# Recurrent layer: the remainder of every second weight chunk by an adding transfer onto a negated copy

## The reference, cut to what matters

```python
def first_block(x, ...):                       # 512 tokens, width 1024, float32
    for i in range(2):
        h = rms_norm(x, norm_g[i])
        x = x + (lru_mixer if i == 0 else fox_mixer)(h, ...)
    return rms_norm(x, final_g)

def lru_mixer(h, w_in, conv_w, conv_b, wa, ba, wx, bx, a_param, w_out):   # the recurrent layer
    u = h @ w_in                               # 1024 -> 2 * 1536
    xb, gate = u[..., :1536], u[..., 1536:]
    xc = causal_depthwise_conv(xb, conv_w, conv_b)               # 4 taps
    r = sigmoid(block_diag_linear(xc, wa, ba)); i = sigmoid(block_diag_linear(xc, wx, bx))
    log_a = -8.0 * r * softplus(-a_param)
    a = exp(log_a); bterm = sqrt(-expm1(2.0 * log_a)) * (i * xc)
    hs = scan(a * previous + bterm)            # over the 512 tokens
    return (hs * silu(gate)) @ w_out           # 1536 -> 1024
```

## Time and profile before

| | |
|---|---|
| median of 3 runs | 2170.46 us |
| profiled execution, its own time | 2171.6 us |
| its span in the trace | 2169.8 us |
| TensorE busy | 2139.7 us (99%) |
| VectorE busy | 1292.5 us (60%) |
| ScalarE busy | 833.5 us (38%) |
| GpSimd busy | 1.4 us |
| queue of SP: 512 KB weight loads, from issue to landing | 3.3 us (median of 389) |

### The profile page before, as it was taken

One profiled execution on the slowest core, in us unless ns is written; L12 is line 12 of the kernel. 1 busy time (PEld: TensorE's weight loads), 2 busy tenths in 40 slices (PEclk: granted clock), 3 DMA queues, 4 the chain that ended last, 5 costly groups with the idle time before them and its releaser, 6 DMA issues.

```text
span 2169.8 us, 27883 instructions
## 1 busy us (share of the span) xinstructions
PE 2139.7 (99%) x10180; PEld 1853.8 (85%) x10190; DVE 1292.5 (60%) x1866; ACT 833.5 (38%) x1162; POOL 1.4 (0%) x6
## 2 busy tenths in 40 slices
PE   9999999999999999999999999999999999999998
PEld 8787878878888888888888888888888888888887
DVE  8878785768665536656553555665446555553545
ACT  5776574645333313233321323443322234222222
POOL 0000000000000000000000000000000000000000
PEclk9999999999999999999999999999999999999998
DMA  5233222213222232333323323222332233233332
GB/s 180 96 108 98 87 78 78 78 64 117 78 89 87 97 104 100 98 106 97 107 90 115 97 97 107 88 78 81 106 105 98 86 111 114 97 97 107 101 102 78
DMA packets 59512, 211.67 MB, mean 98 GB/s; under 512 B 6737, under 2 KB 7121, under 8 KB 59281
## 3 DMA queue, kind: packets, MB, share of 16 engines
q1 hardware_dynamic: 59040, 208.83, 29.4%
q0 software_dynamic: 224, 1.31, 0.2%
q10 hardware_dynamic: 144, 0.12, 0.0%
HBM read 208.14 MB, written 2.10 MB: 97 GB/s over the span
## 4 chain that ended last, share of the span: by engine, by line
PE 81%; DVE 3%; ACT 2%; issue 1%; DVEq 0%; ACTq 0%
PE bank L673 24%; PE bank L675 24%; PE bank L674 24%; PE bank L668 2%; PE bank L669 2%; PE bank L670 2%; PE bank L853 1%; PE bank L903 1%; PE bank L845 1%; ACT arena L1156 1%; ACT arena L1218 0%; DVE w_lo L1382 0%; PE bank L826 0%; PE bank L931 0%; PE bank L827 0%
## 5 line engine op out<-in xcount | busy, mean ns | idle before, releaser
L1382 DVE TENSOR_TENSOR w_lo<-w_raw,w_hi 128x1024 fp32r<-128x1024 f32 x387 | 466.6, 1222 | 682.2 <-ACT w_hi L1002 681.0
L1002 ACT ACTIVATE w_hi<-w_raw 128x1024 fp32r<-128x1024 f32 x387 | 402.6, 1053 | 848.6 <-PE bank L675 812.2
L673 PE MATMUL bank<-h_hi,w_hi 128*128 128x512 f32 x1788 | 683.3, 382 | 8.9 <-DVE w_lo L1382 3.6
L675 PE MATMUL bank<-h_hi,w_lo 128*128 128x512 f32 x1788 | 679.1, 380 | 0.0
L674 PE MATMUL bank<-h_lo,w_hi 128*128 128x512 f32 x1788 | 679.1, 380 | 0.0
L673 PE MATMUL bank<-y_hi,w_hi 128*128 128x512 f32 x1048 | 399.2, 381 | 5.3 <-DVE w_lo L1382 3.4
L674 PE MATMUL bank<-y_lo,w_hi 128*128 128x512 f32 x1048 | 398.1, 380 | 0.0
L675 PE MATMUL bank<-y_hi,w_lo 128*128 128x512 f32 x1048 | 398.0, 380 | 0.0
L673 PEld LDWEIGHTS bank<-h_hi,w_hi 128*128 128x128 f32 x1788 | 339.0, 190 | 60.5 <-DVE w_lo L1382 7.9
L674 PEld LDWEIGHTS bank<-h_lo,w_hi 128*128 128x128 f32 x1788 | 339.1, 190 | 48.6 <-issue 1.4
L675 PEld LDWEIGHTS bank<-h_hi,w_lo 128*128 128x128 f32 x1788 | 338.9, 190 | 47.8
(11 more groups left out here) (236 smaller groups left out, 1494.4 us busy)
## 6 DMA issues: line engine op xcount, KB each, us to landing
w_raw<-in_stream SPq DMA_DIRECT2D x389, 512.0 KB, 3.3
x<-in_x_t SPq DMA_DIRECT2D x8, 256.0 KB, 7.1
out_t<-x SPq DMA_DIRECT2D x8, 256.0 KB, 2.2
arena<-in_consts POOLq DMA_DIRECT2D x1, 1024.0 KB, 5.2
w_raw<-in_stream SPq DMA_DIRECT2D x2, 256.0 KB, 4.5
arena<-in_positions POOLq DMA_DIRECT2D x1, 256.0 KB, 6.0
vec_t<-in_vecs ACTq DMA_DIRECT2D x1, 112.5 KB, 3.3
ident<-in_consts SPq DMA_DIRECT2D x1, 64.0 KB, 6.8
```

What stands on the lines that cost most here:

```text
L673: pe.matmul(out, w_hi[:, slot, w], streamed(a_h), start=first, stop=False)
L675: mm = pe.matmul(out, w_lo[:, slot, w], streamed(a_h), start=False, stop=last)
L1002: A.activation(w_hi[:, slot, :], w_raw[:, slot, :], ACT.Copy).then_inc(hi_ready, 1)
L1382: V.tensor_tensor(w_lo[:, slot, :], w_raw[:, slot, :], w_hi[:, slot, :].bitcast(F32), ALU.subtract).then_inc(lo_ready, 1)
```

## The change

For 18 chunks of the recurrent layer (`ADDED`: 7, 9, 11, ... 41) VectorE makes no remainder. ScalarE, right behind its rounded copy of the chunk, writes a second one with scale -1.0 into `w_lo` ("minus c" below), and counts `minus_ready`. GpSimd waits for that and issues a transfer from `w_raw` to `w_lo` that adds (`accum_op=ALU.add`), so that `w_lo` holds -rounded + raw. TensorE waits for that transfer (`added_in`, a semaphore for each ring slot) where it waited for `lo_ready`; SP, which reloads `w_raw`, does so too. Its first 48 loads are now written out one by one, since their waits differ. The counts of `lo_ready` are lower by the chunks left out.

```diff
+ADDED = range(7, 43, 2)
...
+            single = -(-ADDED.stop // RING) + 1
+            for c in range(RING, single * RING):
+                last = c - RING
+                if last in ADDED:
+                    sp.wait_ge(added_in[c % RING], 16 * transfers(last))
+                else:
+                    sp.wait_ge(lo_ready, last + 1 - sum(a < last for a in ADDED))
+                sp.dma_start(w_raw[:, c % RING, :], stream[c, :, :]).then_inc(raw_loaded[c % RING], 16)
+            with sp.Fori(single, rounds) as r:
...
+            for i, c in enumerate(ADDED):
+                slot = c % RING
+                pool.wait_ge(minus_ready, i + 1)
+                pool.dma_start(w_lo[:, slot, :].bitcast(F32), w_raw[:, slot, :], accum_op=ALU.add)\
+                    .then_inc(added_in[slot], 16)
...
+            def weights_ready(n):
+
+                if by_transfer(T, n):
+                    c = T.fixed["chunk"] + n
+                    pe.wait_ge(added_in[c % RING], 16 * transfers(c))
+                else:
+                    pe.wait_ge(lo_ready, subtracted(T, n + 1))
...
                     A.activation(w_hi[:, slot, :], w_raw[:, slot, :], ACT.Copy).then_inc(hi_ready, 1)
+                    if by_transfer(T, n):
+                        A.activation(w_lo[:, slot, :], w_raw[:, slot, :], ACT.Copy, scale=-1.0)\
+                            .then_inc(minus_ready, 1)
...
                 for n, slot in list(split_slots(T, step))[which]:
 
+                    if by_transfer(T, n):
+                        continue
                     dve.wait_ge(hi_ready, T.value("chunk", n + 1))
```

More of the change, by code:

```diff
@@ L499, in build @@
         hi_ready = sem("hi_ready")
+        minus_ready = sem("minus_ready")
+        added_in = [sem(f"added_in{i}") for i in range(RING)]
         lo_ready = sem("lo_ready")
@@ L534, in norm_banks, with by_transfer, transfers, subtracted @@
             return bank[own], bank[own + 1]
+        def by_transfer(T, n):
+            return not T.loops and T.fixed["chunk"] + n in ADDED
+        def transfers(c):
+            return sum(a <= c and a % RING == c % RING for a in ADDED)
+        def subtracted(T, n):
+            before = sum(T.loops != [] or a < T.fixed["chunk"] + n for a in ADDED)
+            return T.value("chunk", n - before)
         def wait(eng, s, value):
@@ L558, in _ @@
             rounds = (n_chunks + AHEAD) // RING
-            with sp.Fori(1, rounds) as r:
+            single = -(-ADDED.stop // RING) + 1
[7 more added lines that the diff above has]
+            with sp.Fori(single, rounds) as r:
                 for slot in range(RING):
-                    sp.wait_ge(lo_ready, r * RING + (slot - RING + 1))
+                    sp.wait_ge(lo_ready, r * RING + (slot - RING + 1 - len(ADDED)))
                     sp.dma_start(w_raw[:, slot, :], stream[r * RING + slot, :, :])\
@@ L565, in _ @@
             for c in range(rounds * RING, n_chunks + AHEAD):
-                sp.wait_ge(lo_ready, c - RING + 1)
+                sp.wait_ge(lo_ready, c - RING + 1 - len(ADDED))
                 sp.dma_start(w_raw[:, c % RING, :], stream[c, :, :]).then_inc(raw_loaded[c % RING], 16)
@@ L640, in product @@
                     else:
-                        pe.wait_ge(lo_ready, T.value("chunk", c + 1))
+                        weights_ready(c)
                     if step.args.get("apart") and c == step.chunks - 1:
@@ L753, in gates @@
                 pe.wait_ge(a_lo, T.mark["xc", b])
-                pe.wait_ge(lo_ready, T.value("chunk", 1))
+                weights_ready(0)
                 for n in range(4):
```

## The result

| | before | changed |
|---|---|---|
| median | 2170.32 us (2169.27 to 2170.83, 4 runs) | 2181.26 us (2178.2 to 2181.69, 4 runs) |
| profiled execution, its span | 2169.8 us | 2179.7 us |
| VectorE, ScalarE busy | 1292.5, 833.5 us | 1273.2, 850.5 us |

The ratio is 1.0048 (1.0036 to 1.006): slower by 10.9 us, with 2181 predicted. Measured again later beside experiment e9, the same kernel took 2178.57 us (2177.75 to 2180.9, 5 runs; ratio 1.0043, 1.0029 to 1.0057) with a span of 2176.0.

What follows compares the result with a forecast made beforehand. A chain between ScalarE and VectorE, not TensorE, was taken to set the pace from chunk 17 to 39. Chain 4.3, last link 4.9 and clock 1.1 gave +10.3 us, so 2181 us (2179 to 2185, chance 0.52; range 2174 to 2200).

Steps and rivals of the forecast that it cites:

- point 3: Ahead of chunk 17: lo 11 leaves the second convolution's path, -2.2; minus 7 and minus 13 cost +1.9; together -0.3 us.
- point 4: TensorE, late at chunk 17, holds back the next evacuation by some 1 us: +0.9 us.
- Point 1: Negated copies of chunks 17, 23, 27, 33 and 37 are on the chain, 0.96 us each: +4.8 us; others hidden.
- spot (a): Place in a gate round where ScalarE's copies stand directly ahead of Tanh and Exp while VectorE waits, 2.55 us idle.
- Point 2: Subtractions leaving VectorE help only where it is late: -1.0 us at lo 35, -0.1 at 19 and 29 together, others 0.
- D: Time from the negated copy to the landed addition: taken as 5.2 us, carried from 3.3 to 10.4.
- Clock behind chunk 39: TensorE's gap ahead of chunk 39 grows from 3.1 to about 5 us, its clock loss from 1.7 to 2.8: +1.1.
- How D enters: Up to 5.5 us of transfer time only the last link counts, 1 us per us; above 6, about 4 per us.
- short-transfer rival: Transfer time near 3.3 us, since nothing comes from memory: +7.5 us, 2178 us; chance 0.11.
- Long transfer: Rival: the adding transfer takes 6.5 us or more, giving 2186 to 2205 us; chance 0.26.
- VectorE's relief: Rival: relief of VectorE decides, both gaps for `w_lo` and their clock loss go, 11.2 us, 2159 us; chance 0.06.
- Nothing measurable: Rival: the lateness is taken up by TensorE's waits, so no change shows; chance 0.05.

Runs made afterwards that it cites:

- e9: The changed kernel, but chunk 9 is subtracted by VectorE again; 2178.85 us, ratio 1.0036.
- e3: The kernel before, plus ScalarE's eighteen negated copies into an unused tile; no transfers, VectorE subtracts all chunks; 2176.67 us, ratio 1.0032.
- e4: The changed kernel without negated copies and transfers, the eighteen chunks not subtracted either, their remainders left out of the computation; 2160.2 us, ratio 0.9956.
- e6: The changed kernel with a plain transfer in place of the adding one, so the sum is left out; 2174.87 us, ratio 1.0024.
- e7: The changed kernel with adding transfers for chunks 11 and 35 alone; 2166.3 us, ratio 0.9983.
- e2: The changed kernel, but chunk 39 is subtracted by VectorE again; 2172.49 us, ratio 1.0012.
- e1: The changed kernel with an adding transfer for chunk 39 only, all others subtracted by VectorE as before; 2175.0 us, ratio 1.0025.
- e10: The changed kernel unaltered, measured once more; 2178.57 us, ratio 1.0043.
- e5: The changed kernel with a plain transfer to an unused tile, waited for by GpSimd, ahead of each adding one; 2193.95 us, ratio 1.0113.
- e8: GpSimd subtracts chunks 7, 9, ... 37 and 41, with no negated copy or transfer; 39 stays with VectorE; 2170.07 us, ratio 1.0001.

## Why the prediction came out, point by point

The forecast was +10.3 us on the trace, and the trace has +9.9; the place (the end of the chain plus the last transfer) is as foretold. That the sum is so close is in part luck: point 3 came out 1.7 us higher than forecast and point 4 0.9 lower, and the smaller differences of the link and of the rest of the span took off the remainder. One side calculation was wrong.

- **Point 1, five copies at spot (a), +4.8: right.** Tanh moved by 0.94, 0.95, 0.93 and 0.94 us at chunks 23, 27, 33 and 37 and 0.8 at 17; those of 19, 21, 25, 29, 31 and 35 moved nothing. e3 has 4.65 for the section.
- **Point 2, VectorE's relief, -1.0 and -0.1: right.** Where lo 35 is gone the scan's first product comes 1.0 us nearer. e4 shows the same relief worth 3.0 us from 17 to 39 (111.11 against 114.08), but only without the copies: with them it is 117.58 - 118.73 = -1.15.
- **Point 3, ahead of chunk 17, -0.3: failed.** It was +1.4 in the profile that the forecast is held against (+0.2 at the copy of chunk 9, +1.3 from there to chunk 17). The step that failed is "The waits at 77.60 and 96.99 give that back". The 3.53 us at chunk 9 were seen (3.4 forecast), but not the 3.0 us of clock behind it, and together they made TensorE late enough to hold the chain twice: ScalarE's copy of chunk 13 (1.51 us at 64.49) and the evacuation behind it (1.89 us at 78.19). The waits that were to give it back were TensorE's; the chain got nothing back. Against e6, which has the same copies and neither wait, the hold was 3.6 us. The rest of point 3 was too high: without the hold (e6) the section is -2.35 us. lo 11 gave the 2.2 foretold (e7: 2.3), but lo 9, whose departure point 2 put at 0, gave 0.9 more (e9 against e6, and e7's 44.05 against e4's 43.17).
- **Point 4, TensorE late at chunk 17 holds an evacuation, +0.9: right as a mechanism, not paid here.** The 1.04 us wait at 107.61 was covered. e2 pays it (+0.98) because its clock behind the same gap was lower.
- **D, 5.2 us: 4.9.** The link grew by 4.5 instead of 4.9. e1 has the link alone, +4.7.
- **Clock behind chunk 39, +1.1: +1.3.** Its price before was 1.7 us, after 3.0. In the rest of the span nothing was taken up (-0.9, less than the 1.1 us by which the two profiles of the changed kernel differ there). In e10 the stretch behind chunk 39 grew by 0.7 us only, so this term moves too.
- **"How D enters", 1 us per us up to 5.5: failed; about 4 above 6: right.** From the plain transfer's D = 3.2 to 4.9 the time rises 3.7 to 6.4 us over 1.65, some 2 to 4 per us. Chunk 9, wanted at 52.25, is the first that D makes late: at 3.2 it holds nothing (e6), at 4.9 it holds the chain for 1.25 to 3.6 us, which point 3 had at nothing. Above, from 4.9 to 8.1, e5 has 4 to 4.8. The +7.5 for the plain transfer (measured +4.9), and with it the short-transfer rival's 2178, were too high by the rest of point 3 and by the clock behind chunk 39, 0.4 us instead of 1.1.
- **The rivals.** Long transfer: the landing was 5.0 us in the median but 7.7 at most, and a landing 1.1 us later at chunk 9 makes 2.4 of the 3.7 us between the spans of the two profiles. Its 2205 is more than the prediction's own rule gives: 10.3 + 4 x 5.2 for D = 10.4 is +31.1, 2202. VectorE's relief: real, e4 has 2160.2 against the 2159 worked out, but it needs a remainder without ScalarE and without D. Nothing measurable: excluded. A slower VectorE or ScalarE instruction beside a transfer: not seen, a subtraction took 1219 ns on the mean against 1216 before.
- The Trainium skill, in "Collectives: The Full Stack" (The bandwidth ceiling), says that an add in the transfer needs two source reads and halves the rate; the estimate drawn from it was 4.4 us. That estimate was 1.2 us above the plain transfer's by the same pages; the traces have 1.3 (5.0 against 3.7), so the rule fits here as to what the addition adds, and only the plain transfer was priced too low. The row that the prediction found to agree was a load by SP; the 1 MB load by GpSimd took 5.2 us, where the formula that it takes from the Trainium skill, "DMA: Bandwidth & Descriptors" (Anatomy of one DMA), gives an estimate of 4.4.

Settled by the runs: the three costs (copies, link, chunk 9) and their sizes in these profiles. Open: why the last 20 KB of one transfer to chunk 9 come at 14 GB/s for 1.5 us and in another execution do not. Open too: why the clock falls for longer behind one gap than behind an equal one.

## What to carry to other kernels

Find out which engine is the late one at each spot before work is shifted to another: here only some of the 18 subtractions stood on the chain (9, 11, 19, 29, 35 and, as the last link, 39). Taking four of them alone won 6.6 us, and taking all eighteen lost 8 to 11, since five of the copies that paid for them fell on ScalarE just where it was the late one, and since the last link then ended with a transfer. A transfer that replaces a 1.2 us instruction is late by its landing time wherever its user follows within that time, so keep the last link of a chain on an engine. And when an engine's lateness is said to be given back by its idle time, look whether something else waits for its result in between, and add the clock that the gap costs to the lateness.

## What the hardware showed that was not expected

- **The price of the addition.** 512 KB within the core's own memory: 3.7 us from GpSimd's issue to landing plain, 5.0 adding (4.5 to 7.7 over 18). GpSimd was busy 0.53 us per issue plain and 0.86 adding.
- **GpSimd and VectorE get in each other's way by the kind of operands.** Beside GpSimd's subtractions (2.5 us each), VectorE's subtractions and scans, with two inputs from SBUF, took 27% longer on the mean (1219 to 1543 ns, scan 1211 to 1551), the evacuations with one input from PSUM nothing (685 and 684 ns). The mean hides what one pair shows, a subtraction of each in e8:

```profile
144.59 2.38 POOL L604 TENSOR_TENSOR w_lo<-w_raw,w_hi 128x1024 fp32r<-128x1024 f32 x1 [10.66 <-ACT w_hi L1039]
```

```profile
145.42 2.62 DVE L1421 TENSOR_TENSOR w_lo<-w_raw,w_hi 128x1024 fp32r<-128x1024 f32 x1 [4.59 <-ACT w_hi L1039]
```

VectorE's ends 1.07 us behind the end of GpSimd's (148.04 and 146.97), as if it had begun only then; those that overlap none of GpSimd's take 1.2 us. The Trainium skill, in "SBUF — State Buffer" (SBUF: two separate sides), says that a VectorE instruction with two inputs from SBUF and a GpSimd instruction that reads SBUF shut each other out for their whole length; these rows agree.

- **A gap can be worth taking away twice.** Where TensorE waited 0.53 us instead of 3.08 ahead of chunk 39 (e2), the clock behind it stayed at the full level, 2.4 GHz, over the 8 us (1.00 against 0.79), so 4.3 us of a late chain cost 2.7. But equal gaps did not cost equally: behind 4.15 us ahead of chunk 17 it was 0.79 in one kernel and 0.61 in another, and behind gaps of 2.00 us (e7, at 130.26) and 2.14 us (e4, at 101.47) 0.79 and 1.00.
